# Raw weights and low parts 32 bytes into their slots, and tile 0's eviction ahead of a split in the second mixer

## The reference

```python
# first block, twice
x = x + mixers(rms_norm(x, g) @ w_in) @ w_out          # four mixers side by side, 2660 columns
x = x + ffn(rms_norm(x, g))                            # 1024 -> 2 x 2816 -> conv -> gate -> 1024

# second block, four times
x = x + 0.5 * rms_norm_2(swiglu(rms_norm_2(x, g[0]), ff1_w_in[i], ff1_w_out[i]), g[1])
h = rms_norm_2(x, g[2])
m = mixer_a(...) | mixer_b(...) | mixer_c(...)         # by i % 3
x = x + rms_norm_2(m, g[3])
x = x + 0.5 * rms_norm_2(swiglu(rms_norm_2(x, g[4]), ff2_w_in[i], ff2_w_out[i]), g[5])
```

## Time and profile before

| | |
|---|---|
| median of 3 runs | 2537.78 us (2536.23 to 2538.86) |
| the profiled execution | 2536.61 us |
| its span | 2534.8 us |
| TensorE busy | 2518.7 us, 15209 matmuls |
| VectorE busy | 1769.4 us |
| ScalarE busy | 1395.5 us |
| DMA | 459.47 MB, mean 181 GB/s |

### The profile page before, as it was taken

One profiled execution on the slowest core, in us unless ns is written; L12 is line 12 of the kernel. 1 busy time (PEld: TensorE's weight loads), 2 busy tenths in 40 slices (PEclk: granted clock), 3 DMA queues, 4 the chain that ended last, 5 costly groups with the idle time before them and its releaser, 6 DMA issues.

```text
span 2534.8 us, 37208 instructions
## 1 busy us (share of the span) xinstructions
PE 2518.7 (99%) x15209; PEld 2223.5 (88%) x15209; DVE 1769.4 (70%) x2500; ACT 1395.5 (55%) x2078; POOL 150.6 (6%) x228
## 2 busy tenths in 40 slices
PE   9999999999999999999999999999999999999999
PEld 9999888998888988888888888888988888898887
DVE  7778567885775777757657775775777577567773
ACT  7766476664554555545555554554555455455553
POOL 2100011000000000000010000002010000010000
PEclk9999999999999999999999999999999999999999
DMA  7266552664665556556564655655456556563763
GB/s 224 98 178 211 173 166 84 189 194 166 208 196 197 181 162 194 189 187 197 185 221 147 204 192 187 195 187 196 153 166 201 188 180 205 184 207 125 216 189 127
DMA packets 543027, 459.47 MB, mean 181 GB/s; under 512 B 10634, under 2 KB 500058, under 8 KB 542858
## 3 DMA queue, kind: packets, MB, share of 16 engines
q1 hardware_dynamic: 537351, 441.52, 54.9%
q0 software_dynamic: 4656, 15.30, 1.7%
q10 hardware_dynamic: 851, 0.28, 0.0%
HBM read 455.97 MB, written 1.10 MB: 180 GB/s over the span
## 4 chain that ended last, share of the span: by engine, by line
PE 95%; DVE 3%; ACT 1%; DMA 1%; issue 0%; POOL 0%; DVEq 0%; POOLq 0%; ACTq 0%
PE ps L964 28%; PE ps L847 23%; PE ps L846 11%; PE ps L829 5%; PE ps L830 5%; PE ps L831 5%; PE ps L784 2%; PE ps L783 2%; PE ps L782 2%; PE ps L765 2%; PE ps L766 2%; PE ps L767 2%; PE ps L849 1%; PE ps L687 1%; DVE wlo L1956 1%; PE ps L1065 1%
## 5 line engine op out<-in xcount | busy, mean ns | idle before, releaser
L1956 DVE TENSOR_TENSOR wlo<-raw,whi 128x2048 fp32r<-128x2048 f32 (+1 forms) x419 | 956.7, 2287 | 363.2 <-ACT whi L1362 363.1
L1362 ACT ACTIVATE whi<-raw 128x2048 fp32r<-128x2048 f32 (+2 forms) x421 | 800.3, 1906 | 293.2 <-DMA raw<-in_ff_w_out 161.1
L847 PE MATMUL ps<-h,whi 128*128 128x512 f32 x2560 | 873.6, 393 | 0.0
L846 PE MATMUL ps<-h,wlo 128*128 128x256 f32 x2240 | 629.7, 281 | 0.0
L847 PEld LDWEIGHTS ps<-h,whi 128*128 128x128 f32 x2560 | 459.7, 188 | 81.5
L846 PEld LDWEIGHTS ps<-h,wlo 128*128 128x128 f32 x2240 | 421.9, 188 | 15.3
L1362 ACT ACTIVATE u<-ps 128x512 f32<-128x512 f32 x160 | 96.0, 600 | 397.4 <-PE ps L847 397.4
L964 PE MATMUL ps<-whi,hid_hi 128*128 128x512 f32 x880 | 291.3, 390 | 0.0
L964 PE MATMUL ps<-whi,hid_lo 128*128 128x512 f32 x880 | 290.7, 389 | 0.0
L964 PE MATMUL ps<-wlo,hid_hi 128*128 128x512 f32 x880 | 290.3, 389 | 0.0
L829 PE MATMUL ps<-h,whi 128*128 128x256 f32 x1024 | 288.1, 281 | 0.0
(11 more groups left out here) (337 smaller groups left out, 3285.9 us busy)
## 6 DMA issues: line engine op xcount, KB each, us to landing
raw<-in_ff_w_in SPq DMA_DIRECT2D x160, 1024.0 KB, 5.6
raw<-in_ff_w_out SPq DMA_DIRECT2D x88, 1024.0 KB, 4.8
raw<-in_ffn_w_in SPq DMA_DIRECT2D x40, 1024.0 KB, 5.6
raw<-in_a_w_qkv SPq DMA_DIRECT2D x24, 1024.0 KB, 5.0
raw<-in_ffn_w_out SPq DMA_DIRECT2D x22, 1024.0 KB, 4.8
raw<-in_w_in SPq DMA_DIRECT2D x18, 1024.0 KB, 6.2
raw<-in_ff_w_in SPq DMA_DIRECT2D x32, 512.0 KB, 4.4
raw<-in_c_w_qkv SPq DMA_DIRECT2D x12, 1024.0 KB, 5.0
```

The lines of the kernel that those rows point to most:

```text
L846: e.matmul(out[:, 0:SEQ], lo, m.h[:, 0, k, :], start=False, stop=False, skip_group_check=True)
L847: ins = e.matmul(view(out, a=2), hi, m.h[:, :, k, :], start=(k == 0), stop=(k == KT - 1), skip_group_check=True)
L1362: return self.nc.scalar.activation(*a, **k)
L1956: self.e.tensor_tensor(chunk_view(m.wlo[:, slot, :], c), chunk_view(m.raw[:, slot, :], c), chunk_view(m.whi[:, slot, :], c).bitcast(F32), ...
```

## The change

Four things are edited.

1. Two helpers are new: `low_places()` gives each chunk an offset, 8 floats (32 bytes) where the chunk multiplies `h` by columns or heads, 0 for the rows of the output and down projections; `low(a, c)` is chunk c's slot of `raw` or `wlo` from that offset on. All users of `raw` and `wlo` go through it. `whi` keeps its places.
2. Slots of `raw` and `wlo` get 16 floats more (8256 instead of 8192 bytes apart).
3. `behind_h` shrinks from 120 floats to 8. `h` then begins at 117088, again 32 bytes behind a multiple of 64, and `hid` at 133504, 128 bytes lower and again a multiple of 64; everything behind it is 128 bytes lower too.
4. In the second mixer ScalarE waits for each tile's `rstd` by itself, and the split stands between the two evictions.

```diff
+PAD = 16
+LOW_IN = 8
+LOW_SWIGLU = 8
...
-        dst, src = dst_src(self.m.raw[:, c % SLOTS, :], b)
+        dst, src = dst_src(low(self.m.raw, c), b)
...
-                hi, lo = w_of(m.whi[:, c % SLOTS, :], f, k), w_of(m.wlo[:, c % SLOTS, :], f, k)
+                hi, lo = w_of(m.whi[:, c % SLOTS, :], f, k), w_of(low(m.wlo, c), f, k)
...
-        self.act(chunk_view(m.whi[:, slot, :], c), chunk_view(m.raw[:, slot, :], c), ACT.Copy).then_inc(s.split_hi, 1)
+        self.act(chunk_view(m.whi[:, slot, :], c), chunk_view(low(m.raw, c), c), ACT.Copy).then_inc(s.split_hi, 1)
...
-        if l > 0:
-            self.split(0, 0)
-        e.wait_ge(s.rstd, TT * self.rounds["norm"])
         if l == 0:
+            e.wait_ge(s.rstd, TT * self.rounds["norm"])
             keep(0)
             self.split(0, 0)
             keep(1)
         else:
             for t in range(TT):
+                e.wait_ge(s.rstd, TT * (self.rounds["norm"] - 1) + t + 1)
                 self.evict_head(t, proj, C_CQ, HEAD_WIDTH, ACT.Copy)
+                if t == 0:
+                    self.split(0, 0)
...
-        self.e.tensor_tensor(chunk_view(m.wlo[:, slot, :], c), chunk_view(m.raw[:, slot, :], c),
+        self.e.tensor_tensor(chunk_view(low(m.wlo, c), c), chunk_view(low(m.raw, c), c),
                              chunk_view(m.whi[:, slot, :], c).bitcast(F32), ALU.subtract).then_inc(s.split_lo, 1)
...
+def low_places():
+
+    out = []
+    for stage in PLAN:
+        n, rows = chunks_of(stage), 4 if stage[0] in ("mix1", "mix2") else FT // 2
+        out += [LOW_SWIGLU if stage[0] == "swiglu" else LOW_IN] * (n - rows) + [0] * rows
+    return out
+
+
+def low(a, c):
+
+    return a[:, c % SLOTS, LOW_AT[c]:LOW_AT[c] + CW]
...
-            [("raw", [P, SLOTS, CW])],
-            [("wlo", [P, SLOTS, CW], F32R)])
+            [("raw", [P, SLOTS, CW + PAD])],
+            [("wlo", [P, SLOTS, CW + PAD], F32R)])
         sb(ctx, "in_front_of_h", [P, 8])
         m.h = sb(ctx, "h", [P, 2, KT, SEQ], F32R)
-        sb(ctx, "behind_h", [P, 120])
+        sb(ctx, "behind_h", [P, 8])
```

More of the change, by code:

```diff
@@ L518, in start @@
         w = d.w_in[0].rearrange("(k p) c -> p k c", p=P)
-        raw = m.raw[:, 0, :].rearrange("p (k c) -> p k c", k=KT)
+        raw = low(m.raw, 0).rearrange("p (k c) -> p k c", k=KT)
         col, n = IN_PIECES[0][1][0]
@@ L756, in tokens_tile @@
         c = self.c0 + b
-        whi, wlo = (a[:, c % SLOTS, :].rearrange("p (k c) -> p k c", k=KT)[:, :, 0:w] for a in (m.whi, m.wlo))
+        whi, wlo = (a.rearrange("p (k c) -> p k c", k=KT)[:, :, 0:w] for a in (m.whi[:, c % SLOTS, :], low(m.wlo, c)))
         out = m.ps[:, self.bank(b), t * 256:t * 256 + w]
@@ L772, in pair_tile @@
         c = self.c0 + b
-        whi, wlo = (a[:, c % SLOTS, 0:PAIR * w].rearrange("p (k c) -> p k c", k=PAIR) for a in (m.whi, m.wlo))
+        whi, wlo = (a[:, 0:PAIR * w].rearrange("p (k c) -> p k c", k=PAIR) for a in (m.whi[:, c % SLOTS, :], low(m.wlo, c)))
         out = m.ps[:, t, 0:w]
@@ L957, in block @@
         whi = m.whi[:, c % SLOTS, :].rearrange("p (k c) -> p k c", k=2)
-        wlo = m.wlo[:, c % SLOTS, :].rearrange("p (k c) -> p k c", k=2)
+        wlo = low(m.wlo, c).rearrange("p (k c) -> p k c", k=2)
         tok = slice(t * P, (t + 1) * P)
@@ L1395, in split_first @@
         self.e.wait_ge((s.first_landed, s.landed[0])[half], 16)
-        whi, raw = (chunk_view(a[:, 0, :], 0)[:, 4 * half:4 * half + 4, :] for a in (m.whi, m.raw))
+        whi, raw = (chunk_view(a, 0)[:, 4 * half:4 * half + 4, :] for a in (m.whi[:, 0, :], low(m.raw, 0)))
         self.act(whi, raw, ACT.Copy).then_inc((s.first_hi, s.split_hi)[half], 1)
@@ L2051, in split_first @@
         self.e.wait_ge((s.first_hi, s.split_hi)[half], 1)
-        whi, wlo, raw = (chunk_view(a[:, 0, :], 0)[:, 4 * half:4 * half + 4, :] for a in (m.whi, m.wlo, m.raw))
+        whi, wlo, raw = (chunk_view(a, 0)[:, 4 * half:4 * half + 4, :] for a in (m.whi[:, 0, :], low(m.wlo, 0), low(m.raw, 0)))
         self.e.tensor_tensor(wlo, raw, whi.bitcast(F32), ALU.subtract).then_inc((s.first_lo, s.split_lo)[half], 1)
@@ L3094 @@
 NARROW = narrow_chunks()
+LOW_AT = low_places()
 def build(nc, d):
```

## The result

The changed kernel takes **2558.8 us** (median of 4, 2558.6 to 2559.4) against 2537.3 (4 runs, 2536.2 to 2538.9): a ratio of **1.0085** (95% interval 1.0067 to 1.0102). It is slower, where 2521.3 us was forecast, and lies outside the range. The profiled execution has a span of 2556.8 us, 22.0 more than before.

A forecast was written before the change was run, and what follows sets the result against it. TensorE, 99% busy at full clock, was the bound, through the start-to-start matmul distance. Gains of 10.3 + 2.8 + 1.6 + 1.8 = 16.5 us took 2536.6 to 2520.1, plus 1.2 for the median: 2521.3 us; range 2507 to 2549.

The forecast's parts named there:

- part 3: Wider slots and everything behind `h` 128 bytes lower: down projections keep 226.7 ns, out projections unchanged, cost 0.
- C: Rival: down projections lose their rate, 226.7 towards 233 ns, + 16.6 us, giving 2538; chance 0.07.
- Part 1: Low parts 32 bytes in become like-placed with `h`: gains of 10.3, 2.8 and, in `pair_tile`, 1.6 us.
- The wide term: In `wide_chunk`, loads of `wlo` while 512 columns stream: 10.3 us gained, bounds 0 to 10.3.
- The term for `features_chunk` and `tokens_tile`: Matmuls of 256 columns beside loads of `wlo`: 2.8 us gained, half of 5.6, ends 0 and 5.6.
- rival B: Like places collide where the load has no slack: 17.5 us paid again, less 1.8, giving 2553.5; chance 0.14 in full.
- Part 2: Raw weights 32 bytes in: DMA writes, ScalarE copy and VectorE subtraction start elsewhere but stay hidden, cost 0.
- Part 4: Second mixer: tile 0's eviction moved to the split's place removes TensorE's wait, 1.8 us gained.
- Rival A: Place is not the cause of the 3 to 7 ns; only the mixer's wait goes, giving 2536; chance 0.12.

The follow-up runs named there:

- a_hid_128_lower: The kernel before with only `hid` and all that lies behind it 128 bytes lower: 2552.6 us, ratio 1.0067.
- c_after_hid_back: The changed kernel with `hid` put back at its byte place of before: 2551.6 us, ratio 1.0060 against the kernel before.
- b_h_320_higher: The kernel before with `h` alone 320 bytes higher, where the changed kernel has it: 2551.5 us, ratio 1.0059.
- f_all_low_32: The kernel before with all raw weights and low parts 32 bytes higher, slots still 8192 bytes apart: 2542.5 us, ratio 1.0023.
- m1_swiglu_256: The changed kernel with slots 256 bytes wider, `h` and `hid` at 32 and 0, offset for SwiGLU chunks alone: 2526.6 us, ratio 0.9956 against the kernel before.
- m2_all_256: As m1_swiglu_256, but with the low offset for all chunks that multiply `h`: 2527.9 us, ratio 0.9963 against the kernel before.
- g_h_at_0: The kernel before with `h` at a multiple of 512 bytes, so every operand begins at 0: 2543.4 us, ratio 1.0026.
- e_mixer_alone: The kernel before with the second mixer's edit alone, nothing moved in memory: 2535.1 us, ratio 0.9992.
- d_stride_alone: As c_after_hid_back, with the low parts' and raw weights' offset at 0 everywhere: 2552.4 us, ratio 1.0062 against the kernel before.

## Why the prediction was wrong

**The step that failed is part 3, "Slots 64 bytes wider, everything behind `h` 128 bytes lower", cost 0.** It rested on the reading that only the place in a 64-byte line counts, taken from two places, 0 and 32; no row held an operand at 64 or 128. Measured: `hid` 128 bytes lower is 14.7 us by itself (a_hid_128_lower) and 6.7 in the change; the slots' steps of 64 bytes are 6.4 (c_after_hid_back); together +13.1. And the part left out `h`: it moved from 32 to 352, "the same place in a line", which is 32 to 96 of 256 and costs 13.8 us by itself in `features_chunk` and `wide_chunk` (b_h_320_higher). The mechanism stood among the rivals, as C: it named `hid`, the slots and a price of 16.6 us (13.1 measured). It got a chance of 0.07 on the ground that 246 down matmuls run over all slots at one rate; but those slots differ by 8192 bytes, a multiple of 256, so the rows couldn't speak to it. C also priced only the down projections, and set them against a gain that the same moves had destroyed. A gain of 16.5 us was forecast and the span grew by 22.0; of the 38.5 us between them some 13 are the down projections, 14 `wide_chunk` and 9 `features_chunk` with `tokens_tile`.

**Part 1, the low parts.** The wide term was 10.3 us. Where the places are kept it is 8.2 (f_all_low_32 and m1_swiglu_256), from 231.7 to 228.3 ns, where 226.7 was taken: right in kind, a fifth of it missing. In the change itself it is gone, since `h` at 96 meets `wlo` at four different places (32, 96, 160 and 224; slots 0 and 4 have the same one). The term for `features_chunk` and `tokens_tile`, a gain of 2.8, has the wrong sign: from m1_swiglu_256 to m2_all_256, which moves the low parts of these chunks (and of the `pair_tile` chunks outside the SwiGLU stages), it is +1.7 and -0.4 us. `pair_tile` gains 0.8 in m2_all_256 against before, of 1.6 forecast. In m1_swiglu_256 it gains 0.3, and only in the eight SwiGLU stages, where its low parts are moved: streaming `wlo` there takes 228.4 to 231.7 ns instead of 232.4 to 233.0. Half of rival B is true for this reason: like-placed operands of 256 columns do cost 120 ns (g_h_at_0), its very number; its price of 17.5 us assumed the same of 512 columns, and there they gain.

**Part 2, raw weights.** Right. The split takes 2286 and 1907 ns as before. The landing of a 1 MB input chunk went from 5.6 to 6.1 us, and nobody waits for it.

**Part 4, the mixer.** 1.8 us forecast, 1.6 measured in the span (e_mixer_alone): the wait went, and 0.4 us for `wlo` came in. The sum looked only at the subtraction of the split that is pushed back, 0.7 us late by its account, and that one is covered as it said. It left out the subtraction before it, which ended at 333.88 already and became what TensorE waits for once the eviction was early.

**Rival A** falls. Moving `hid` alone, with every instruction and pattern left as it was, changes the time by 0.67%. The Trainium skill ("SBUF — State Buffer", section "Who interferes with whom") has TensorE's two read ports as independent; the runs disagree, by 5 ns on a matmul of 512 columns, also where no other engine and no transfer is at work (226.7 against 232.5 ns). How the reads meet isn't visible in a trace: the rule stated here is one of addresses, and its cause stays open. Open too is why a matmul's distance depends on its neighbours (`whi` streaming with `hid` loaded, both unmoved, takes 227.3 ns before and 229.2 in c_after_hid_back, where only the `wlo` between has moved), and why the halves alternate in g_h_at_0. `h` was tried at 0, 32 and 96 only, and `hid` at 0 and 128; other places may be better still.

## What to carry to other kernels

Where TensorE is busy 99% at full clock, read the distance from start to start, and treat the byte place of both operands as a parameter of the kernel. Padding one tile moves everything behind it: move by multiples of 256 bytes, or put the neighbours back, or the gain at one place is paid for at three others. A rule read from two places in the rows is no rule for a third; the cheapest test here was one pad changed by 32 floats.

## What the runs showed of the hardware

- With a weight load for each matmul, the distance depends on where both operands begin, modulo 256 bytes: 227 to 234 ns for 512 columns, 117 to 121 ns for 256 (the means of the table, fp32r, full clock). A move of three tiles by 256 bytes gave 0.9999, and two slots 256 bytes apart in place gave 227.4 and 228.3 ns where the other three gave 230 to 234.5 (c_after_hid_back).
- With all operands at 0, 512 columns of a weight row are fastest (226.8 ns) and 256 columns of `h` take a steady 120 ns; with `h` at 32 and the weights at 0 the latter take 116 to 119. `wlo` and `h` both at 32 with `whi` at 0 gave 231.5 ns for the 512 columns, so the places of the neighbours count too.
- Input chunks of 1 MB land in 6.1 instead of 5.6 us where they are written 32 bytes in, and in 6.0 where the slots go in steps of 64 bytes without an offset (d_stride_alone).
